# Moving the local attention of a three-mixer block from the mixing stage into the projections

## The reference

```python
h = rms_norm(x, pre_gain) * (1.0 + scale) + shift
proj = h @ w_in                                    # 1024 x 3088
(aq, ak, av, ag, rq, rk, rv, rg, gq, gk, gv, gg, ga) = jnp.split(proj, IN_SPLITS, axis=-1)
aq, ak = apply_rotary(aq, ...), apply_rotary(ak, ...)
a_out = sliding_window_attention(aq, ak, av, sinks) * jax.nn.silu(ag)
r = retention(rq, rk, rv)                          # rq, rk rotated too
r_out = rms_norm(r) * jax.nn.silu(rg)
log_a = jax.nn.log_sigmoid(ga @ gla_gate_w + gla_gate_b) / 16
g = gated_linear_attention(gq, gk, gv, log_a)
g_out = rms_norm(g, gla_norm_gain) * jax.nn.silu(gg)
y = jnp.concatenate([a_out, r_out, g_out], axis=-1) @ w_out
return x + gate * rms_norm(y, post_gain)
```

## Time and profile before

| | us |
|---|---|
| median of 3 runs (2091.52 to 2093.15) | 2092.64 |
| span of the profiled execution | 2085.9 |
| PE busy | 1982.1 (95%) |
| DVE busy | 1089.9 (52%) |
| ACT busy | 933.0 (45%) |
| projections, layer 0 and 1 (57.0 to 188.6, 378.5 to 510.1) | 131.6 each |
| mixing, layer 0 (188.6 to 297.3) | 108.7 |
| mixing, layer 1 (510.1 to 615.1) | 105.0 |
| a 512 KB transfer of `w_mod`, issue to landing (median) | 4.6 |

### The profile page before, as it was taken

The page is one execution under the profiler, slowest core; times in us unless marked ns, Lnnn a source line. Parts: engine busy times, 40 slices in busy tenths (PEclk is TensorE's granted clock), DMA queues, the critical chain, the costliest instruction groups (busy, mean ns, idle before and its releaser), DMA issues.

```text
span 2085.9 us, 25306 instructions
## 1 busy us (share of the span) xinstructions
PE 1982.1 (95%) x9881; PEld 1482.8 (71%) x9881; DVE 1089.9 (52%) x2023; ACT 933.0 (45%) x1737; POOL 12.7 (1%) x28
## 2 busy tenths in 40 slices
PE   8999889999889999889999999999999999999997
PEld 3876446777456888566788888777666668888885
DVE  5623964622874322757655543442386575555333
ACT  3733764643664333574432222344587443223223
POOL 1000000000000000000000000000000000000000
PEclk8999999999989999999999999999999999999999
DMA  8331432223203433003233333425400123333331
GB/s 289 118 92 51 162 101 81 71 71 83 81 21 87 147 92 92 8 2 116 74 98 101 92 93 100 110 54 125 146 2 2 51 71 101 101 92 99 94 95 47
DMA packets 301267, 183.13 MB, mean 88 GB/s; under 512 B 17550, under 2 KB 292108, under 8 KB 299948
## 3 DMA queue, kind: packets, MB, share of 16 engines
q1 hardware_dynamic: 295437, 166.05, 27.6%
q10 hardware_dynamic: 4704, 13.31, 1.7%
q0 software_dynamic: 1008, 2.15, 0.3%
HBM read 179.22 MB, written 2.27 MB: 87 GB/s over the span
## 4 chain that ended last, share of the span: by engine, by line
PE 85%; DVE 8%; ACT 4%; issue 1%; DMA 1%; ACTq 0%; DVEq 0%; SPq 0%
PE PS L911 22%; PE PS L913 22%; PE PS L912 22%; PE PS L1057 3%; PE PS L1085 3%; PE PS L1070 2%; PE PS L1211 1%; DVE WLO L2088 1%; ACT WHI L1523 1%; PE PS L1234 1%; PE PS L1243 1%; DVE X L2055 1%; PE PS L1129 1%; PE PS L1150 1%; PE PS L1138 1%
## 5 line engine op out<-in xcount | busy, mean ns | idle before, releaser
L912 PE MATMUL PS<-LO,WHI 128*128 128x512 f32 x1690 | 660.3, 391 | 0.0
L911 PE MATMUL PS<-HI,WHI 128*128 128x512 f32 x1578 | 626.5, 397 | 26.5 <-DVE LO L2061 9.2
L913 PE MATMUL PS<-HI,WLO 128*128 128x512 f32 x1578 | 617.0, 391 | 0.0
L2088 DVE TENSOR_TENSOR WLO<-RING,WHI 128x1024 fp32r<-128x1024 f32 (+3 forms) x271 | 314.4, 1161 | 532.6 <-ACT WHI L1523 531.6
L1523 ACT ACTIVATE WHI<-RING 128x1024 fp32r<-128x1024 f32 (+3 forms) x271 | 272.6, 1007 | 471.9 <-PE PS L913 450.1
L911 PEld LDWEIGHTS PS<-HI,WHI 128*128 128x128 f32 x1578 | 297.8, 189 | 109.4 <-issue 27.2
L912 PEld LDWEIGHTS PS<-LO,WHI 128*128 128x128 f32 x1690 | 319.0, 189 | 64.8 <-issue 1.2
L913 PEld LDWEIGHTS PS<-HI,WLO 128*128 128x128 f32 x1578 | 297.7, 189 | 63.2
L911 PE MATMUL PS<-HIDDEN,WHI 128*128 128x512 f32 x352 | 137.1, 389 | 0.6 <-PE PS L913 0.6
L912 PE MATMUL PS<-HIDDEN,WHI 128*128 128x512 f32 x352 | 137.0, 389 | 0.0
L913 PE MATMUL PS<-HIDDEN,WLO 128*128 128x512 f32 x352 | 136.9, 389 | 0.0
(11 more groups left out here) (346 smaller groups left out, 2355.8 us busy)
## 6 DMA issues: line engine op xcount, KB each, us to landing
RING<-in_ffn_w_up SPq DMA_DIRECT2D x88, 512.0 KB, 3.8
RING<-in_w_in SPq DMA_DIRECT2D x48, 512.0 KB, 3.9
RING<-in_w_mod SPq DMA_DIRECT2D x32, 512.0 KB, 4.6
RING<-in_ffn_w_down SPq DMA_DIRECT2D x32, 512.0 KB, 4.0
RING<-in_ev_w_in SPq DMA_DIRECT2D x30, 512.0 KB, 3.9
RING<-in_w_out SPq DMA_DIRECT2D x16, 512.0 KB, 4.6
RING<-in_od_w_in SPq DMA_DIRECT2D x15, 512.0 KB, 4.0
RING<-in_ffn_w_down SPq DMA_DIRECT2D x16, 384.0 KB, 3.4
```

The lines of the kernel that those rows point to most:

```text
L911: mm(bank, WHI[i2][:, i, :], hi, start=(k == 0), stop=False)
L912: mm(bank, WHI[i2][:, i, :], lo, start=False, stop=False)
L913: return mm(bank, WLO[i2][:, i, :], hi, start=False, stop=last)
L2088: tt(WLO[i2][:, 0:nk, :], raw, WHI[i2][:, 0:nk, :], ALU.subtract).then_inc(me.signals(w_split), 1)
```

## The change

The local attention leaves the mixing stage. In "proj" a new job kind W is one slot of `swa_lane` on PE, ACT and DVE. `with_window` puts such a slot behind each feature from the seventh on (`FIRST_BESIDE = 7`) and behind the job of the gate logits; what is left of 20 slots stands at the end. The steps of a pair are now a slot or more apart on each engine: PE has in slot i the scores of pair i, the transposes of pair i-3 and the values of pair i-4.

To make room, the value feature of the attention moves from the eleventh to the sixth job; the lane's scores, transposes and values use PSUM banks 4 to 7; exponentials are taken in place in `PAIR_S` (four buffers); the result goes to the query tiles `AQ`; the halves for the rotation move to the tiles of `AG`, and the first silu waits until they are used. In mixing only `state_lane` is left. Its gating of the attention (`gated`) moves on DVE from the end to the two slots of retention masks 4 and 5, and the order of its end is new: the last `weigh` after the retention output, the low halves of the four attention inputs ahead of the first weights. ACT makes four input halves at once instead of three. Several gla buffers have new places. The pieces below are, in this order: the job list, `with_window`, the constants, PE's lane, ACT's silu, ACT's lane, DVE's lane, DVE's retention steps, and `mixers` (shown for DVE, alike on PE and ACT).

```diff
+            jobs += turned_jobs([feat(w, 640, src, z(AV))]
+            jobs += [feat(w, 768, src, z(AG), how="silu", first=True)]
+            return with_window(woven(jobs))
...
+        def with_window(jobs):
+            got, slots, n_feature = [], WINDOW_SLOTS, 0
+            for j in jobs:
+                n_feature += j["kind"] == "F"
+                got.append(j)
+                if j["kind"] == "G" or j["kind"] == "F" and n_feature >= FIRST_BESIDE and slots:
+                    got.append(dict(kind="W", chunks=[]))
+                    slots -= 1
+            return got + [dict(kind="W", chunks=[])] * slots
...
+        WINDOW_SLOTS, FIRST_BESIDE = 20, 7
...
+                for i in range(WINDOW_SLOTS):
+                    if i < len(todo):
+                        scores(i)
+                    if 0 <= i - 3 < len(todo):
+                        turn(i - 3)
+                    if i >= 4:
+                        values(i - 4)
                     yield
...
+                        if "first" in j:
+                            act.wait_ge(halves_used, 9 * (l + 1))
...
+                for i in range(WINDOW_SLOTS):
+                    if i == 1:
+                        act.preload_act_table_set(LN_EXP)
+                    if 0 <= i - 1 < len(todo):
+                        exps(i - 1)
+                    if 0 <= i - 2 < len(todo):
+                        normalise(i - 2)
+                    if i >= 4:
+                        mixed(i - 4)
+                    if 0 <= i - 3 < len(todo):
+                        collect(i - 3)
                     yield
...
+                for i in range(WINDOW_SLOTS):
+                    if 0 <= i - 1 < len(todo):
+                        scaled(i - 1)
+                    if 0 <= i - 2 < len(todo):
+                        recips(i - 2)
                     yield
...
                 masked(4)
+                gated(0)
+                gated(1)
                 masked(5)
+                gated(2)
+                gated(3)
...
-                window, state = swa_lane(l), state_lane(l)
-                for _ in range(MIX_SLOTS):
-                    next(window)
-                    next(state)
-                    next(window)
-                for _ in state:
+                for _ in state_lane(l):
                     pass
```

More of the change, by code:

```diff
@@ L964, in linear @@
                     if j["kind"] == "N":
+                        continue
+                    if j["kind"] == "W":
+                        next(lane)
                         continue
@@ L1002, in linear @@
                                     n_taken += n
+                                if k == total // 2 and j.get("beside"):
+                                    next(lane)
                                 ins = products(bank, i2, i, k, k == total - 1, j["src"])
@@ L1531, in _, with linear @@
             n_gelu, n_halves = [0], [0]
-            def linear(jobs, l, tail=None, late=None, hold=False, early=False, three=False, to_three=False, loads=None):
+            def linear(jobs, l, tail=None, late=None, hold=False, early=False, three=False, to_three=False, loads=None, lane=None):
                 n, upto = 0, at_split[0] + sum(len(j["chunks"]) for j in jobs if j["kind"] == "F") if hold else len(chunks)
@@ L1563, in linear @@
                         act.preload_act_table_set(LN_EXP)
+                    if j.get("beside"):
+                        next(lane)
                     bank = take()
@@ L2088, in weights, with linear @@
                     tt(WLO[i2][:, 0:nk, :], raw, WHI[i2][:, 0:nk, :], ALU.subtract).then_inc(me.signals(w_split), 1)
-            def linear(jobs, l, tail=None, hold=False, three=False, to_three=False):
+            def linear(jobs, l, tail=None, hold=False, three=False, to_three=False, lane=None):
                 n, upto = 0, at_split[0] + sum(len(j["chunks"]) for j in jobs if j["kind"] == "F") if hold else len(chunks)
@@ L2401, in state_lane @@
                 yield
-                weigh(NB - 1)
-                weights(at_split[0] + 1)
-                low(0, H[:, 0, :], None)
-                weights(at_split[0] + 2)
-                if len(GROUPS[l]) > 1:
-                    modulated(1)
-                for k in (1, 2):
-                    low(k, H[:, k, :], None)
-                gated(3)
                 for _ in range(2):
@@ L2416, in state_lane @@
                     tt(H[:, 4 + t, :], z(RG + t), RET_RS[:, t, :], ALU.mult).then_inc(me.signals(normed), 1)
-                for k in (3, 4, 5):
+                weigh(NB - 1)
+                for k in range(4):
+                    low(k, H[:, k, :], None)
+                weights(at_split[0] + 1)
+                if len(GROUPS[l]) > 1:
+                    modulated(1)
+                weights(at_split[0] + 2)
+                for k in (4, 5):
                     low(k, H[:, k, :], None)
```

151 lines of the change are left out of this document (57 added, 94 removed).

## The result

| | before | after |
|---|---|---|
| median | 2092.08 us (4 runs, 2091.06 to 2093.15) | 2107.32 us (4 runs, 2106.56 to 2109.10) |
| ratio, 95% interval | | 1.0083 (1.0069 to 1.0097) |
| span of the profiled execution | 2085.9 us | 2107.3 us |

The change makes the kernel slower: 15.2 us by the medians, 17.4 by the ratio, 14.4 to 20.3 by its interval. I had forecast 2096.2, no change that can be measured. The time lies in my range, 2086 to 2108, but well outside the forecast's own, 2091 to 2100.

A forecast was written before the change was run, and what follows sets the result against it. PE was taken to bound the projections and DVE's gated-linear row mixing. Projections +50.2 us less mixing gains of 46.6 gave +3.6 on a span of 2085.9; with 6.7 for the median, 2096.2 us, range 2086 to 2108.

The forecast's parts named there:

- What bounds the kernel: Both stages: PE is full in the projections; DVE's row of gated-linear work paces mixing, a bare round 12.6 us.
- Inside a dense stream such pieces are a little cheaper: Projections: the lane's pieces cost less between products, 0.11 us off per slot, so 24.6 instead of 26.4 us per layer.
- the discount of 1.8: Projections: amount taken off the lane's 26.4 us per layer, from transposes costing 0.47 in the stream, 0.58 in mixing.
- the last collect: End of projections: a short hop between PE and ACT for the last values, uncovered, 0.5 us per layer.
- the dear end: Projections: no discount at all, 26.4 us per layer; the other end was 21.1, discounting each of three pieces.
- Table loads: Projections: 13 more ACT function-table loads per layer fit in the slots of 7.1 us and cost nothing.
- the small rival: Projections, small form of rival 3: 0.3 us more per table switch makes ACT bind, some +1.5 per layer; chance 0.06.
- Mixing, layer 1: Layer 1 from PE's first mixing matmul to its resumption in the output projection: 83.5 us with clock, gain 23.5.
- The clock: Mixing: PE's idle times lower its granted clock, adding 3 us to layer 1 and 1 to layer 0.
- Rival 2: Mixing: low clock rules once near sums come over 4 us late; +9 us in all, 2102; chance 0.20.
- Their last step reuses a slot of the ring ... lands some 5.7 us later and takes half a microsecond: Layer 0 mixing, next layer's modulation rows: slot freed at t = 71, last step ends at 77.4, resumption at 87.5.
- the clock's 1 us: Layer 0 mixing: 1 us added for PE's low clock, less than layer 1's 3 because modulation steps fill the gaps.

The follow-up runs named there:

- e3_kept_busy: Changed kernel with unused full-width products where PE idles in mixing, mostly layer 1, two in layer 0; 2104.52 us, ratio 1.0065.
- e5_small_rows: Changed kernel with each transfer of modulation rows cut from 512 KB to 64 KB, PE's row products kept; single run 2104.07 us.
- e1_visits: Changed kernel with eight small unused pieces on PE ahead of features 3 to 6 of both projections; single run 2114.05 us.
- e7_turns_first: Changed kernel with transposes first in each lane visit to PE, then scores, then values; single run 2102.35 us.

## Why the prediction was wrong

**What bounds the kernel: right.** PE was full in the projections at clock 1.00, and DVE's row paces mixing: with the lane gone its rounds were 12.7 us, forecast 12.6.

**Projections: the wrong step, "Inside a dense stream such pieces are a little cheaper".** I took the discount from the only small piece that the stream held, the transposes, and gave it to scores and values. The sum of the pieces by their own prices, 26.4 us, was right: from the starts of the pieces to the next product I read 24.6 us more than before in the visits and 1.7 at the end, 26.3. What it left out is:

- the discount of 1.8, which does not exist for a visit: +1.7. What I read as a discount of the stream was a change of shape that the transposes did not make there
- the borders, 17 visits of which five already had a transpose: +2.95 (30.5 less all else). This is the fourth change of a full visit, on the way back to the products, which no piece's price from mixing has in it
- one wait for ACT in the short slots at the end: +0.6
- the last collect: 0.6 in place of 0.5, as forecast

together 5.4 us per layer, 10.7 of the 15.9 by which the stages of the two profiles miss the sum; by the medians I missed 11.1. The sign of a bound was wrong as well: I had called 26.4 the dear end, and excluded, without a row for it, that a piece could cost more inside the stream than outside. The earlier trace rows showed transposes between products, and no row showed scores or values there.

**Table loads: right.** I costed them at nothing, with 1.5 us per layer as the small rival; it is 0.8, of which 0.6 is the wait listed above. The drain of 1.38 us that the Trainium skill's "ScalarE: Activation LUTs", section "What ACT_TABLE_LOAD costs", adds to each switch is not there: 13 loads in layer 0's projections have 0.2 us of idle time ahead of them in all, and what they would have held back is not held back. By that page the sum would have been 29 us higher; the trace decides, and it has 1.6.

**Mixing, layer 1: right within 1 us.** First block's end t = 31.2 (30.3), fourth 70.3 (68.1 without the clock), resumption 84.4 (83.5).

**The clock: right in kind, a little large.** 2.4 us (e3_kept_busy) where I had 3. Rival 2, which needed sums over 4 us late, did not come about: DVE waited 0.93 us.

**Mixing, layer 0: the wrong step, "Their last step reuses a slot of the ring ... lands some 5.7 us later and takes half a microsecond".** By this term the last step ended at t = 77.4. It ended at 81.9 (303.84, where ACT starts to copy its rows), and it had waited for no transfer: PE came to it late, and the landing was not the bound. This 4.5 us is the miss of layer 0; what is behind it took 0.8 more than I had and the clock's 1 us is not there. Two things were missing. PE waits for transfers in the middle of the stage, which in the longer stage of before cost nothing visible (1.4 us of waits, the blocks at 38.9 and 54.2 in both layers): 2.4 us in this profile, by e5_small_rows. And at the end not one step but five stand on PE between the near sums and the last values, with the output weights behind them in the ring. I had priced a step at 0.5; by the timeline of PE five of them (four records each) take 4.66 us, 0.93 each. They stood there in the trace of before as well, and I had not read them (before, then after):

```profile
284.82 1.89 PE L1211 MATMUL PS<-RING,TINY 128*32 128x512 f32 x8
...
289.27 2.77 PE L1211 MATMUL PS<-RING,TINY 128*32 128x512 f32 x12
```

```profile
297.15 1.89 PE L1226 MATMUL PS<-RING,TINY 128*32 128x512 f32 x8
...
301.02 2.77 PE L1226 MATMUL PS<-RING,TINY 128*32 128x512 f32 x12
```

Shortening a stage by 19 us does not shorten what its transfers need, nor the steps that stand behind its last block.

**The chances.** I gave 0.40 to no change and 0.44 to slower. Three errors had one sign; that the pieces are dearer in the stream was in none of the rivals. That the time still lies within 2086 to 2108 is luck: the upper part of that range stood for a low clock that rules in mixing, which did not come about.

## What to carry over

Small pieces put into a dense stream of products cost their own time and, here, about 0.2 us for every change of the shape in which the array is used, the one back to the stream included; the price of a piece that keeps the shape does not hold for one that changes it. Count the changes, not only the pieces, and let the piece that keeps the array's shape come first. Work is worth moving out of a stage that waits only as far as it costs there: the same lane added 30.5 us to a full PE and took 19 to 23 from a stage where part of it lay in others' shadow. And a stage that is shortened keeps its transfers: look at which of them were hidden by its length.

## What the runs showed of the hardware

- A satisfied semaphore wait ahead of a matmul cost nothing that the trace shows (0.83 and 0.84 us, 0.45 and 0.45).
- Each change between the shapes 128*128, 64*128 and 128*64 cost about 0.2 us at full clock: 0.38 to 0.41 left over for two (e1_visits), 0.77 for four (after), 0.60 for three (e7_turns_first, with the same instructions in another order). Full-array pieces of four or eight records between the products left over 0.01.
- In e3_kept_busy PE stood idle for 2.3 us between 592 and 596, and the granted clock was 0.50 from 596 to 598: the fillers lifted the mean of layer 1's mixing from 0.86 to 0.95, not to 1.
- Executions of one kernel differ by up to 4.6 us before the third feature starts, more than several of the effects above.
